# A fused decoder layer on one core: sums of sixteen w_down pairs are made ahead in the up stage, the convolution's third tap moves to ScalarE, and w_down has 22 merged pairs, 14 of them in its second half

## The reference

```python
h = rms_norm(x, ffn_norm_g)
u = causal_depthwise_conv(h @ w_up, conv_w, conv_b)   # width 3, w_up 2048 x 11264
gate, val = jnp.split(u, 2, axis=-1)                  # 5632 each
x = x + (jax.nn.silu(gate) * val) @ w_down            # w_down 5632 x 2048
```

## Time and profile before

| | |
|---|---|
| median of the timed runs | 1435.23 us |
| the profiled execution | 1435.17 us, its span 1433.3 us |
| PE busy | 1427.8 us (100%) |
| weight load of PE busy | 1222.9 us (85%) |
| DVE busy | 1138.3 us (79%) |
| ACT busy | 841.5 us (59%) |
| POOL busy | 448.0 us (31%) |
| moved by transfers | 272.25 MB, 190 GB/s |

### The profile page before, as it was taken

The page is one execution under the profiler, slowest core; times in us unless marked ns, Lnnn a source line. Parts: engine busy times, 40 slices in busy tenths (PEclk is TensorE's granted clock), DMA queues, the critical chain, the costliest instruction groups (busy, mean ns, idle before and its releaser), DMA issues.

```text
span 1433.3 us, 23700 instructions
## 1 busy us (share of the span) xinstructions
PE 1427.8 (100%) x7626; PEld 1222.9 (85%) x7626; DVE 1138.3 (79%) x1503; ACT 841.5 (59%) x1181; POOL 448.0 (31%) x493
## 2 busy tenths in 40 slices
PE   9999999999999999999999999999999999999999
PEld 7888888888888888888888888888888888888887
DVE  6778998886656566899967778777778778999998
ACT  7545667666767666666664455455554545465553
POOL 2310000333132213650025455655556555200000
PEclk9999999999999999999999999999999999999999
DMA  8565665655554545567555565566665565566664
GB/s 260 187 197 172 209 195 186 193 176 176 161 162 160 167 170 178 189 221 234 192 178 184 183 202 181 186 191 190 190 191 185 180 198 185 192 232 206 204 207 148
DMA packets 121063, 272.25 MB, mean 190 GB/s; under 512 B 10688, under 2 KB 10976, under 8 KB 121008
## 3 DMA queue, kind: packets, MB, share of 16 engines
q1 hardware_dynamic: 119936, 268.99, 58.1%
q0 software_dynamic: 896, 2.42, 0.6%
q10 hardware_dynamic: 176, 0.14, 0.0%
HBM read 269.42 MB, written 2.10 MB: 189 GB/s over the span
## 4 chain that ended last, share of the span: by engine, by line
PE 99%; DMA 0%; DVE 0%; DVEq 0%; issue 0%
PE bank L2098 98%; PE bank L2152 1%; DMA y<-in_x 0%; PE bank L2371 0%; PE bank L2412 0%; DVE y L1770 0%; PE bank L2235 0%; PE bank L2171 0%; PE bank L2213 0%; DVE y L1815 0%; DVEq L201 0%; PE bank L2220 0%; PE bank L2210 0%; PE bank L2202 0%; DVEq L529 0%
## 5 line engine op out<-in xcount | busy, mean ns | idle before, releaser
L1100 DVE TENSOR_TENSOR lo<-raw,hi 128x1024 fp32r<-128x1024 f32 (+1 forms) x342 | 444.3, 1304 | 167.0 <-ACT hi L639 166.3
L639 ACT ACTIVATE hi<-raw 128x1024 fp32r<-128x1024 f32 (+1 forms) x342 | 359.2, 1053 | 271.6 <-PE bank L2098 266.9
L2098 PE MATMUL bank<-h2T,hi 128*128 128x512 f32 x1408 | 483.3, 394 | 0.0
L2098 PE MATMUL bank<-h2T,lo 128*128 128x256 f32 x1408 | 376.8, 278 | 0.0
L2098 PEld LDWEIGHTS bank<-h2T,hi 128*128 128x128 f32 x1408 | 257.9, 188 | 53.5
L2098 PE MATMUL bank<-hT,hi 128*128 128x512 f32 (+1 forms) x784 | 272.9, 395 | 0.0
L2098 PEld LDWEIGHTS bank<-h2T,lo 128*128 128x128 f32 x1408 | 264.4, 188 | 7.8
L2098 PE MATMUL bank<-hT,lo 128*128 128x256 f32 (+1 forms) x784 | 212.6, 281 | 0.0
L2062 POOL TENSOR_TENSOR u<-u,rms_row 128x256 f32<-128x256 f32 x88 | 120.9, 1374 | 184.7 <-DVE u L1621 165.7
L2098 PE MATMUL bank<-hi,ffT 128*128 128x512 f32 x576 | 177.4, 389 | 0.0
L2098 PEld LDWEIGHTS bank<-hT,hi 128*128 128x128 f32 (+1 forms) x784 | 143.9, 187 | 29.4
(11 more groups left out here) (292 smaller groups left out, 2017.6 us busy)
## 6 DMA issues: line engine op xcount, KB each, us to landing
raw<-in_w_up SPq DMA_DIRECT2D x176, 512.0 KB, 3.5
raw<-in_w_in SPq DMA_DIRECT2D x160, 512.0 KB, 3.4
raw<-in_w_down SPq DMA_DIRECT2D x88, 512.0 KB, 4.4
raw<-in_w_branch SPq DMA_DIRECT2D x32, 512.0 KB, 3.6
raw<-in_w_out SPq DMA_DIRECT2D x24, 512.0 KB, 4.6
raw4h<-in_w_in SPq DMA_DIRECT2D x8, 512.0 KB, 3.4
raw5h<-in_w_in SPq DMA_DIRECT2D x8, 512.0 KB, 4.4
raw45m<-in_w_out SPq DMA_DIRECT2D x8, 512.0 KB, 4.9
```

The costliest lines, as they stand in the source:

```text
L639: act.activation(hi[s][:, 0:width], raw[s][:, 0:width], ACT.Copy)\
L1100: dve.tensor_tensor(lo[s][:, 0:width], raw[s][:, 0:width], hi[s][:, 0:width].bitcast(f32), ALU.subtract)\
L2098: return pe.matmul(o, l, r, start=start, stop=stop, skip_group_check=True)
```

## The change

In the up stage, groups 1 to 8, SP loads one pair of w_down (pairs 8 to 15) for each half into a buffer `pre[m]`, DVE makes the three sums there (`pre_sums`), and SP stores the buffer to a tensor `sums` in memory. In w_down these pairs are `stored` steps: merged steps whose third and fourth chunk are loaded from `sums` like weights (four loads in place of two, the first half as wide). Six more pairs (0 to 5) are merged in the second half only, their sums made by DVE in w_down. So 22 steps are merged, eight in the first half and fourteen in the second, where the turns are plain, stored, merged with sums made there. Where such a step stands behind a stored one, its sums are made within the stored one (`down_summed(i, step, after)`). There are seven batches in place of five, at new places, and two of the six raw buffers lie elsewhere and are used from an earlier load on. The third tap of the convolution is made by ACT, with the value's bias in the same instruction (`last_tap`); POOL keeps the product with the norm and the one with the silu.

```diff
-    BATCHES = [Batch(8, 2, (1, 1), (2, 0), (2, 1), (3, 1), (4, 0)),
-               Batch(10, 2, (5, 0), (5, 1), (6, 0), (6, 1), (7, 0)),
-               Batch(12, 2, (9, 0), (10, 2), (12, 2), (13, 0), (14, 2)),
-               Batch(0, 2, (19, 0), (19, 1), (20, 0), (21, 0), (21, 1)),
-               Batch(2, 2, (25, 2), (27, 2), (29, 2), (30, 0), (31, 2))]
+               Batch(10, 2, (4, 1), (5, 2), (6, 0), (6, 1), (7, 2)),
...
+               Batch(2, 2, (28, 1), (29, 2), (30, 2), (31, 0), (31, 1)),
+               Batch(4, 2, (33, 2), (34, 0), (34, 1), (35, 2), (36, 2))]
     SUMMED = [b.pair + j for b in BATCHES for j in range(b.count)]
+    STORED_AT, STORED = 8, 8
...
-        first = [(0, k, None) for k in range(8)]
-        for i in range(6):
-            first += [(0, SUMMED[i], i), (0, 14 + i, None)]
-        first += [(0, k, None) for k in (20, 21)]
-        rest = [k for k in range(PAIRS) if k not in SUMMED]
-        second = [(1, rest[0], None)]
-        for i in range(10):
-            second += [(1, SUMMED[i], i), (1, rest[i + 1], None)]
-        second += [(1, rest[11], None)]
+        first = [(0, k, None) for k in range(5)]
+        for i, k in enumerate((5, 6, 7, 16, 17, 18, 19, 20)):
+            first += [(0, SUMMED[i], i), (0, k, None)]
+        first += [(0, 21, None)]
+        second = [(1, k, SUMMED.index(k) if k in SUMMED else None)
+                  for k in (6, 8, 0, 7, 9, 1, 16, 10, 11, 17, 12, 2, 18, 13, 3, 19, 14, 4, 20, 15,
+                            5, 21)]
...
-    WIDE_FROM = 20
+    WIDE_FROM = 8
+    LOADS = [(s, k) for s in STEPS for k in range(4 if s.stored else 2)]
...
+            def pre_load(m, n):
+
+                wait_alone(sp, pre_stored[m], 16 * n - 15)
+                row, col = 2 * P * n + 2 * P * (STORED_AT - 1), m * BLOCK
+                sp.dma_start(pre[m][:, 0:2 * GRP], w_down[ds(row, P), col:col + BLOCK])\
+                    .then_inc(pre_landed[m], 16)
...
+            def pre_store(m, n):
+
+                wait_alone(sp, pre_summed, 6 * n - 3 + 3 * m)
+                sp.dma_start(sums[ds(P * n + (m * STORED - 1) * P, P), :], pre[m][:, :])\
+                    .then_inc(pre_stored[m], 16)
...
+            with sp.Fori(2, STORED + 1) as n:
+                up_loads(n, {(0, 0): lambda: pre_load(0, n), (0, 4): lambda: pre_store(1, n - 1),
+                             (1, 0): lambda: pre_load(1, n), (1, 4): lambda: pre_store(0, n)})
...
+            def last_tap(b, n, ct):
...
+                act.wait_ge(scaled, e + 1)
+                tap = params[:, ds(2 * KT + 2 * FT * 2 + b * FT + e, 1)]
+                if b == 0:
+                    act.activation(conv[b][ct % 2][:, :], u[b][ct][:, 2:S + 2], ACT.Copy,
+                                   scale=tap).then_inc(done, 1)
...
+                if j in (1, 3, 5, 7):
+                    last_tap(1, n - 1, j // 2)
...
+                    if storing and j in (1, 2, 3, 9, 10, 11):
+                        pre_sums(j // 8, n, j % 8 - 1)
...
+            def down_summed(i, step, after):
                 down_lo(step.chunk, weights(step.raw), GRP)
                 down_lo(step.chunk + 1, weights(step.raw + 1))
+                if step.stored:
+                    down_lo(step.chunk + 2, weights(step.raw + 2))
+                    if after is not None:
+                        sums13(after)
+                    between(i, 2)
+                    down_lo(step.chunk + 3, weights(step.raw + 3))
+                    if after is not None:
+                        sums24(after)
+                    return
                 down_lo(step.chunk + 2, sum13)
                 between(i, 2)
                 down_lo(step.chunk + 3, sum24)
```

More of the change, by code:

```diff
@@ L69, in hybrid_layer @@
     C_ROWS = KT // TAIL_CK
-    Step = namedtuple("Step", "m pair made chunk raw")
+    Step = namedtuple("Step", "m pair made chunk raw stored", defaults=(False,))
     S_BLOCKS = range(2, NB)
@@ L508, in hybrid_layer @@
         far_copied = sem("far_copied")
+        pre_landed = [sem(f"pre_landed{m}") for m in range(2)]
+        pre_summed = sem("pre_summed")
+        pre_stored = [sem(f"pre_stored{m}") for m in range(2)]
         y_summed = sem("y_summed")
@@ L591, in _ @@
                 load_step(step, w_out, (step.m - NB) * BLOCK)
-            with sp.Fori(0, NU) as n:
-                for b in range(2):
-                    load_group(C_UP + b * CPG, w_up, 2 * CPG * n, b * FF + GRP * n)
-            for i, step in enumerate(STEPS):
-                for k in range(2):
-                    q = step.raw + k
-                    old = RAW_BEFORE[q]
-                    if old is None and q < SLOTS:
-                        wait_alone(sp, lo_done, C_DOWN + q - AHEAD)
-                    elif old is None:
-                        wait_alone(sp, ffT_done, FT)
-                    else:
-                        was = STEPS[old // 2]
-                        wait_alone(sp, lo_done, was.chunk + old % 2 + 1)
-                        if was.made is not None:
-                            wait_alone(sp, (sum13_done, sum4_done)[old % 2],
-                                       len(ROW_S) + S_COUNT[was] + 1)
-                    kt = 2 * step.pair + k
-                    load(RAW_SLOT[q], raw_down[RAW_SLOT[q]][:, :],
-                         w_down[kt * P:(kt + 1) * P, step.m * BLOCK:(step.m + 1) * BLOCK])
+            def pre_load(m, n):
[3 more added lines that the diff above has]
+                    .then_inc(pre_landed[m], 16)
+                sp.dma_start(pre[m][:, 2 * GRP:3 * GRP],
+                             w_down[ds(row + P, P), col + GRP:col + BLOCK])\
+                    .then_inc(pre_landed[m], 16)
+                sp.dma_start(pre[m][:, 3 * GRP:4 * GRP], w_down[ds(row + P, P), col:col + GRP])\
+                    .then_inc(pre_landed[m], 16)
@@ new lines, in _ @@
+            for m in range(2):
+                wait_alone(sp, pre_stored[m], 16 * STORED + 1)
+            with sp.Fori(STORED + 2, NU) as n:
+                up_loads(n, {})
+            for q, (step, k) in enumerate(LOADS):
+                slot, old = RAW_SLOT[q], RAW_BEFORE[q]
+                if old is None and q < SLOTS:
+                    wait_alone(sp, lo_done, C_DOWN + q - AHEAD)
+                elif old is None:
+                    wait_alone(sp, w_used, C_DOWN)
+                else:
+                    was, part_ = LOADS[old]
+                    wait_alone(sp, lo_done, was.chunk + part_ + 1)
+                    if was in S_COUNT:
+                        wait_alone(sp, (sum13_done, sum4_done)[part_],
+                                   len(ROW_S) + S_COUNT[was] + 1)
+                width = GRP if step.stored and k == 0 else BLOCK
+                if k < 2:
+                    kt = 2 * step.pair + k
+                    src = w_down[kt * P:(kt + 1) * P, step.m * BLOCK:step.m * BLOCK + width]
+                else:
+                    row = (step.m * STORED + step.pair - STORED_AT) * P
+                    src = sums[row:row + P, (k - 2) * BLOCK:(k - 1) * BLOCK]
+                load(slot, raw_down[slot][:, 0:width], src)
@@ L1053, in left_hi_part @@
                 if pair < 8:
-                    act.wait_ge(w_used, STEPS[pair + 1].chunk + 2)
+                    act.wait_ge(w_used, [s for s in STEPS if s.pair == pair + 1][0].chunk + 2)
                 act.activation(ff_pairs(pair, 2)[:, :, 0, 0, P:S], left_raw[b][:, :, 0, :],
@@ L1656, in gate_step, with up_body @@
                     neighbours(0, n, j // 2)
[L1658 removed]
+            def up_body(n, before, storing=False):
                 for j in range(2 * CPG):
```

125 lines of the change are left out of this document (83 added, 42 removed).

## The result

The changed kernel takes 1439.65 us (median of seven runs, 1438.57 to 1441.99), the kernel before 1435.26 beside it (seven runs, 1435.18 to 1436.13): ratio 1.0030, 95% interval 1.0020 to 1.0039. It is slower by 4.4 us, 0.3%, where I had forecast no change. The time lies in the range (1431.9 to 1441.5) but above the forecast's own band (1433.5 to 1438.1), in the part above it that I had given to late sums with 0.13, and on the slower side of the 0.2% bound, to which I had given 0.27; 1436.7 was 3 us too low. The profiled execution is the fastest of the seven, 1438.57 us, so its span accounts for 3.5 of the 4.4 us.

What follows compares the result with a forecast made beforehand. PE was taken to bound the kernel, busy 1427.8 of 1433.3 us. Terms -4.1 - 0.2 + 2.5 + 0.6 + 1.5 + 1.2 = +1.5 gave 1436.7 us, no change; range 1431.9 to 1441.5.

Steps and rivals of the forecast that it cites:

- the forecast's own band: Whole kernel: time between 1433.5 and 1438.1 us, given a chance of 0.58.
- late sums: w_down's second half: merged steps' raws land late, so their sums are late; 0.13 for this up to 1441.5 us.
- the 0.2% bound: Whole kernel: under 0.2%, 2.9 us, a measurement can't tell a difference from nothing; slower than that had 0.27.
- What leaves PE: w_down: 18 fewer matmuls on PE, 990 in place of 1008, at 0.227 us each: -4.1 us.
- the first half's late chunk: w_down's first half: a chunk that was late should be in time with its sums gone from DVE: -0.2 us.
- The merged step behind a stored one: w_down's second half: the merged step's second chunk is late by 0.41 us in each of six pairs: +2.5 us.
- Work put into M: Seventh batch's two pieces in merged steps 33 and 36 make the fourth lo late: 0.7 + 0.8 = +1.5 us.
- Late landing: w_down's second half: the first sum may wait for its raw; 0.1 us a pair, +0.6, ends 0 and 8.1.
- Rival 2: w_down's second half: raws land late and the sums with them, 1440 to 1444 us; chance 0.20.
- The end: After w_down's last matmuls: one plain step instead of two behind the last merged one, DVE's additions finish later: +1.2 us.
- up, 0: Up stage: added sums, taps, loads and stores all hide beside PE, stores landing in 7.9 us: 0 us.
- the four adds: First plain step of w_down's second half: adds of the first half's results fall where DVE is idle, costing nothing.

Runs made afterwards that it cites:

- experiment 1: Changed kernel with the second half's turn reordered from plain, stored, merged to plain, merged, stored: 1434.79 us, ratio 0.9999 to the kernel before.
- experiment 2: Changed kernel with the seventh batch's two pieces moved from merged steps 33 and 36 into plain steps 31 and 37: 1439.13 us, ratio 1.0027.
- Experiment 3: Changed kernel whose second-half loads of stored sums take 128 columns in place of 1024, with as many transfers and waits: 1437.66 us, ratio 1.0015.
- experiment 5: Changed kernel with second half ordered plain, merged, stored, two plain steps at the end, batch pieces moved and three additions put off: 1439.72 us, ratio 1.0033.
- experiment 7: Changed kernel with one plain step moved to the very end, merged still behind stored, batch pieces one step earlier: 1440.80 us, ratio 1.0042.
- experiment 10: The kernel of experiment 5 with the batches' pieces at other places, whole in steps 26 and 32: 1434.56 us, ratio 0.9995.
- experiment 6: The kernel of experiment 5 with the third tap and the value's bias back on GpSimd: 1464.04 us, ratio 1.0202.
- experiment 12: The kernel of experiment 6 with VectorE's additions in up cut to 64 columns, all transfers and waits kept: 1442.48 us, ratio 1.0049.
- experiment 4: Changed kernel without up's pair loads, additions and stores; stored steps read rows of w_down instead: 1438.66 us, ratio 1.0024.
- experiment 9: The order of experiment 1 with batch pieces and the additions of the first half's results placed elsewhere: 1433.60 us, ratio 0.9987.

## Why the prediction was right, and where its size was off

The mechanism was right: PE loses in w_down's second half by waiting for DVE's lo, in the places that I had named, and the end grows. What was off is the size, and with it the forecast of no change: 4.4 us are clear of nothing. By terms, in the profiled execution:

- **What leaves PE, -4.1 and -0.2:** held. The matmuls number 18 fewer and the first half's late chunk is gone.
- **The merged step behind a stored one, +2.5:** 2.4 us. The second chunks of steps 24, 36, 39 and 42 are late by 0.38 to 0.40 with nothing else near, and experiment 1 removes them; pairs 27 and 33 have the same 0.4 beside a late landing.
- **Work put into M, +1.5:** 1.4 (0.7 in step 33, 0.75 in 36). In experiment 2 they are gone from these chunks, but its median gives back only 0.5, and where the rest went is shown by one profile alone.
- **Late landing, +0.6 ("I take 0.1 a pair"):** this is the term that was mis-sized: 2.1 us in this execution, in steps 27 and 32 with 33; the sums' waits for raws were 3.3 us. I took the median of landings in the kernel before, at 187 GB/s, and the new stretch moves 230 to 265; and I walked one load, where SP sends the merged step's two and the next plain step's in 4 us. I also had DVE through with the plain step's second chunk 0.28 us after PE began the step; at step 31 it took 1.1 us, so the raw left 0.8 us later than in the pairs 27 and 42, and then took 6.3 us to land. The longest landing rose from 6.5 to 7.2 with the median almost unchanged. Rival 2 named the place; its price of 3.9 to 8.1 us for late sums was not reached. Experiment 3 gives 2 us between the medians for the transfers' part (0.8 between the profiles' waits).
- **The end, +1.2:** 1.5 (3.56 to 5.03 us). Experiments 5 and 7 bring it back with a second plain step, and lose more elsewhere; with the pieces placed better (experiment 10) the same order loses 2.9 us less in w_down than experiment 5.
- **up, 0:** held to 0.02 us at w_down's start, with landings of 5.8 to 7.5 us for the stores, under my 7.9 and far from the 11.1 at which SP would have held the loads. That this term came out was in part luck: I had counted the tap's move as free in both directions, and it is what makes the additions free: on GpSimd it costs 21 us in up (experiments 6 and 12). With additions and no tap on GpSimd PE does not wait in up (the changed kernel), with the tap and no additions none (the kernel before), nor with no additions and the tap on ScalarE (experiment 4).
- **Not foreseen:** `sub_u3` behind step 30 makes the next plain chunk 0.3 late. I placed "the four adds" and overlooked the three that follow.

The sum of the profile: -4.1 - 0.2 + 2.4 + 1.4 + 2.1 + 0.3 + 1.5 = +3.4, beside the 3.5 of the spans. So without the mis-sized landings (+1.5) and the piece not foreseen (+0.3) the span would have come out as forecast, 1.5 to 2 us over the kernel before. Another 0.9 us lies between this execution and the median of the seven. Some of it may be landings: the spread was 3.4 us here against 1.0. Some of it may lie ahead of all that was changed: in the profiles here up's first matmul starts between 708.6 and 709.8 us, and in this one at 708.93. No profile of a slower execution of this kernel was kept, and it stays open.

Why does it gain nothing, then? The 4.1 us saved on PE are there, as experiment 9 shows: its span is 1430.7, 2.6 under the kernel before, and the end is 1.3 us longer there and 0.6 us of waits are left. The changed kernel spent them on DVE's lateness in six short windows (2.4 us), on raws that landed late (2.1), on two pieces put into merged steps (1.4) and on the end (1.5).

## What to carry to other kernels

A share of 90% says little; what counts is what stands between the last free buffer and the next chunk that is due. Where steps of different length take turns, put the extra work behind the step with the longest chunks, and look at each step whose chunks are short. Where a buffer ring feeds several engines in order, a piece that one engine makes and the next consumes needs a step between the two (in experiment 5, where both stood in one step, it cost 2.2 us at one chunk), and an engine that was left idle on average may still be the one whose chain a neighbour waits for in line.

## What the runs showed of the hardware

GpSimd's and VectorE's operations stretch each other, in both directions. For GpSimd's side compare experiments 6 and 12, which differ only in the length of VectorE's additions in up: with the short ones GpSimd's third tap took 705 ns in place of 927 and its product with the silu 808 in place of 900, while its product with the norm went from 1326 to 1376 and the bias stayed at 1439 (the tap's group, 740 to 1200 us, experiments 6 and 12):

```profile
L2169 POOL TENSOR_TENSOR conv<-u,params 128x256 f32<-128x256 f32 x78 | 72.3, 927 | 13.0 <-POOL u L2166 12.1
```

```profile
L2169 POOL TENSOR_TENSOR conv<-u,params 128x256 f32<-128x256 f32 x83 | 58.5, 705 | 13.9 <-POOL u L2166 13.0
```

A mean depends on what VectorE runs just then. The product with the norm took 1392 ns in the kernel before and 997 in the changed one, the product with the silu 787 and 1395; in both kernels the operation that stands right behind VectorE's taps is a slow one, the bias before (1437) and the product with the silu now. That is read from the rows and was not tested by itself (before, then changed, 750 to 1190 us):

```profile
L2062 POOL TENSOR_TENSOR u<-u,rms_row 128x256 f32<-128x256 f32 x79 | 110.0, 1392 | 113.8 <-DVE u L1621 101.9 <-ACT silu L982 11.9
L2079 POOL TENSOR_TENSOR conv<-conv,params 128x256 f32<-128x256 f32 x40 | 57.5, 1437 | 57.2 <-DVE conv L1631 57.2
```

```profile
L2161 POOL TENSOR_TENSOR u<-u,rms_row 128x256 f32<-128x256 f32 x80 | 79.7, 997 | 208.3 <-DVE u L1700 208.3
L2175 POOL TENSOR_TENSOR conv<-conv,silu 128x256 f32<-128x256 f32 x40 | 55.8, 1395 | 101.6 <-DVE conv L1710 101.6
```

For VectorE's side: its additions of 1024 columns took 1409 ns in up in the changed kernel and 1658 in experiment 6, where GpSimd has the tap and the bias as well, against 1223 for the same form in w_down's second half of the changed kernel, where GpSimd was idle (the group of experiment 6):

```profile
L1754 DVE TENSOR_TENSOR pre<-pre 128x1024 f32<-128x1024 f32 x16 | 26.5, 1658 | 0.0
```

The Trainium skill (GPSIMD Engine Reference, Specifications) has the two share their SBUF interfaces for instructions with two SBUF inputs; these rows agree. The sizes are what the runs add: 15% and 36% on VectorE's addition, 31% on GpSimd's tap.
